# Gathering experts' tokens by an indirect transfer from GpSimd instead of by matmuls with one-hot columns

## The reference

```
scores = softmax(xf @ router_w)                      # 384 tokens, 16 experts
best_group = argmax(sum of the 2 best in each group of 4)
idx = top_k(scores inside the best group, 2)         # two experts per token
gates = scores[idx] / sum(scores[idx])
for each expert e, over the tokens sent to it (x):
    y = (silu(x @ w1[e]) * (x @ w3[e])) @ w2[e]      # three 1024 x 1024 matrices
out[token] += gate * y
```

## Time and profile before

| | |
|---|---|
| median of 3 runs | 1675.11 us |
| the profiled execution, its own time | 1676.27 us |
| its span in the profile | 1674.5 us |
| mean granted TensorE clock | 0.972 |
| busy: PE / DVE / ACT / POOL | 93% / 43% / 20% / 0% |
| DMA | 495.66 MB, mean 296 GB/s |
| chain that ended last | PE 83%, DVE 6%, DMA 5%, ACT 3%, issue 2% |

### The profile page before, as it was taken

The page is one execution under the profiler, slowest core; times in us unless marked ns, Lnnn a source line. Parts: engine busy times, 40 slices in busy tenths (PEclk is TensorE's granted clock), DMA queues, the critical chain, the costliest instruction groups (busy, mean ns, idle before and its releaser), DMA issues.

```text
span 1674.5 us, 21517 instructions
## 1 busy us (share of the span) xinstructions
PE 1555.0 (93%) x7910; PEld 699.9 (42%) x7911; DVE 713.3 (43%) x2050; ACT 331.6 (20%) x539; POOL 0.2 (0%) x4
## 2 busy tenths in 40 slices
PE   6999999978999999999989799896999998999996
PEld 3454555543343333333333355453333333333333
DVE  3325665352424434334343548725334342434343
ACT  4322222030101111010101357413011110111111
POOL 0000000000000000000000000000000000000000
PEclk9999999989999999999999899997999999999998
DMA  9438776830858999999968501424799995999993
GB/s 351 153 106 299 264 262 226 349 153 1 354 249 336 423 422 422 422 422 422 422 267 350 201 0 51 201 101 163 288 413 422 422 422 240 423 422 421 423 423 132
DMA packets 83949, 495.66 MB, mean 296 GB/s; under 512 B 4465, under 2 KB 21121, under 8 KB 28225
## 3 DMA queue, kind: packets, MB, share of 16 engines
q1 hardware_dynamic: 82432, 489.33, 72.3%
q10 hardware_dynamic: 1472, 5.72, 1.0%
HBM read 493.45 MB, written 1.58 MB: 296 GB/s over the span
## 4 chain that ended last, share of the span: by engine, by line
PE 83%; DVE 6%; DMA 5%; ACT 3%; issue 2%; SPq 0%; DVEq 0%; ACTq 0%
PE PS L752 81%; DMA halves<-in_moe_w 4%; PE PS L756 2%; DMA halves<-in_ada_w 1%; DVE misc L1760 1%; ACT hT L543 1%; DVE xc L1702 1%; DVE misc L1522 0%; DVE halves L1522 0%; DVE halves L1513 0%; DVE halves L1515 0%; DVE halves L1514 0%; DVE hT L1750 0%; ACT hT L528 0%; ACT hT L514 0%
## 5 line engine op out<-in xcount | busy, mean ns | idle before, releaser
L752 PE MATMUL PS<-halves,hT 128*64 128x512 f32 x3072 | 677.0, 596 | 22.4 <-ACT hT L543 17.2
L752 PEld LDWEIGHTS PS<-halves,hT 128*64 128x64 f32 x3072 | 225.4, 137 | 442.5 <-issue 432.8
L752 PE MATMUL PS<-hT,halves 128*128 128x384 f32 x640 | 218.7, 497 | 8.4 <-ACT halves L626 6.5
L1702 DVE SCALAR_TENSOR_TENSOR xc<-PS,MOD,xc 128x128 f32<-128x128 f32 x592 | 195.8, 409 | 37.4 <-PE PS L752 37.4
L752 PEld LDWEIGHTS PS<-hT,halves 128*128 128x128 f32 x640 | 121.5, 193 | 106.7 <-issue 23.0
L1750 DVE TENSOR_TENSOR hT<-hT,PS 128x512 f32<-128x512 f32 x32 | 22.0, 688 | 279.3 <-ACT hT L528 279.3
L752 PE MATMUL PS<-halves 128*128 128x384 f32 (+1 forms) x336 | 118.5, 512 | 0.7 <-ACT pre L573 0.7
L752 PE MATMUL PS<-h,hT 128*64 128x512 f32 x408 | 108.8, 667 | 7.4 <-issue 3.9
L1760 DVE COPY misc<-PS 128x512 f32<-128x512 f32 x32 | 22.1, 692 | 216.6 <-PE PS L752 216.6
L528 ACT ACTIVATE hT<-PS 128x512 f32<-128x512 f32 x32 | 19.1, 597 | 449.6 <-PE PS L752 449.6
L752 PE MATMUL PS<-hT,misc 64*128 64x384 f32 x512 | 91.2, 495 | 3.6
(11 more groups left out here) (232 smaller groups left out, 1107.5 us busy)
## 6 DMA issues: line engine op xcount, KB each, us to landing
halves<-in_moe_w SPq DMA_DIRECT2D x192, 2048.0 KB, 16.4
halves<-in_ada_w SPq DMA_DIRECT2D x48, 1024.0 KB, 6.9
halves<-in_hy_w_in SPq DMA_DIRECT2D x12, 1024.0 KB, 5.2
halves<-in_rg_w_in SPq DMA_DIRECT2D x4, 2048.0 KB, 15.5
halves<-in_hy_w_out SPq DMA_DIRECT2D x4, 1024.0 KB, 8.2
halves<-in_rg_w_out SPq DMA_DIRECT2D x2, 2048.0 KB, 9.7
halves<-in_rg_wa SPq DMA_DIRECT2D x1, 2048.0 KB, 11.4
halves<-in_rg_wx SPq DMA_DIRECT2D x1, 2048.0 KB, 15.2
```

The source lines that it names most:

```text
L752: return nc.tensor.matmul(out, lhsT, rhs, start=start, stop=stop)
L1702: ins = v.scalar_tensor_tensor(xc[:, k, cs], PS[:, bank, cs], MOD[:, l, 8 * G2 + k, s:s + 1], xc[:, k, cs], ALU.mult, ALU.add)
```

## The change

Four things are changed, all in the mixture of experts.

**The gather.** At the start of each layer GpSimd stores `h` in a tensor in HBM, `tokens`, in rows of 512 values (2 KB), two rows per token. For experts 1 to 16 of a layer the six gather matmuls are gone. In their place TensorE does three matmuls of `pick`, now 128 wide (the 64 slots twice), with a constant column that holds twice each token's number; VectorE adds 1 on the upper 64 partitions and converts to integers (two instructions of one column); and GpSimd starts an indirect transfer that reads the 128 named rows into `xg`. TensorE's `xg` transposes wait for that transfer (`xg_in`) instead of for VectorE's copy. For each layer's expert 0 the matmul gather stays.

**First and third matrices in fours.** The loads of w1 and w3 take four matrix rows for each partition, contiguous in HBM (16 KB), where they took two blocks of two rows (8 KB). The channels of a token are stored in `tokens` in the order that this needs: ScalarE's `token_tile` writes them permuted. The bytes are the same, and w2 is loaded as before.

**Further passes' outputs in eight banks.** The eight combine matmuls of a further pass go to eight different banks and wait for no addition in between (they wait for `hid`, which frees banks 2 and 3). After them TensorE waits for the fourth addition or a later one (`8 * n + 5`), where it waited for the second or a later one; and the wait for all eight additions stands before the base pass's combine matmuls, no longer before the `hid` transposes.

**`w13_last`** is now counted up by the first of the three small matmuls.

```diff
-        pick = cut(hT, 0, NT * BASE).rearrange("p (t r) -> p t r", t=NT)
+        pick = stack[:, 0, :].rearrange("p (t r) -> p t r", t=NT)
+        rows_f = stack[:, 1, 0:1]
+        rows_i = stack[:, 1, 1:2].bitcast(mybir.dt.uint32)
+        tokens = [nc.dram_tensor(f"tokens{l}", (2 * N, HALF), F32, kind="Internal").ap() for l in range(LAYERS)]
...
-                w = {m: A[m].rearrange("l e (k p j) n -> p (l e) k (j n)", p=P, j=2) for m in ("moe_w1", "moe_w3", "moe_w2")}
+                w = {m: A[m].rearrange("l e (k p j) n -> p (l e) k (j n)", p=P, j=j)
+                     for m, j in (("moe_w1", 4), ("moe_w3", 4), ("moe_w2", 2))}
...
+                    a.activation(h[:, i // 2, i % 2 * HALF:i % 2 * HALF + HALF].rearrange("p (k c) -> p k c", k=4),
+                                 PS[:, 2 + i, :].rearrange("p (c k) -> p k c", k=4), ACT.Copy).then_inc(S("tok"), 1)
...
+        @block.gpsimd
+        def _(pool_):
+            for l in range(LAYERS):
+                for t in range(NT):
+                    pool_.wait_ge(S("tok"), before("tok", l) + 2 * t + 2)
+                    pool_.dma_start(tokens[l][2 * P * t:2 * P * t + 2 * P, :].rearrange("(p j) c -> p (j c)", j=2),
+                                    h[:, t, :]).then_inc(S("tok_out"), 16)
+                pool_.wait_ge(S("tok_out"), 16 * NT * (l + 1))
+                for e in range(NE):
+                    pool_.wait_ge(S("rows"), before("rows", l) + e + 1)
+                    pool_.wait_ge(S("xT_mm"), before("xT_mm", l) + e + 1)
+                    pool_.indirect_dma_start(xg, None, tokens[l], bass.IndirectOffsetOnAxis(rows_i, 0)) \
+                        .then_inc(S("xg_in"), 16)
...
                     pe.wait_ge(S("x_gpT"), n + 1)
-                    for i, (k, bank) in enumerate(X_COMBINE):
+                    pe.wait_ge(S("hid"), before("hid", l) + e + 1)
+                    for k, bank in X_COMBINE:
                         g, kk = k // 2, k % 2
-                        if i >= 6:
-                            pe.wait_ge(S("x_acc"), 8 * n + i - 2)
                         mm(PS[:, bank, 0:N], Xyo[...], XgpT[...], True, True).then_inc(S("x_c_mm"), 1)
-                    pe.wait_ge(S("x_acc"), 8 * n + 3)
+                    pe.wait_ge(S("x_acc"), 8 * n + 5)
...
-                        gather(l, 0, 2, pick, HALF, S("w13_last")).then_inc(S("G_mm"), 1)
+                        for t in range(NT):
+                            last = mm(PS[:, 0, 0:1], pick[:, t, :], const("token_rows")[:, t:t + 1], t == 0, t == NT - 1)
+                            if t == 0:
+                                last.then_inc(S("w13_last"), 1)
+                        last.then_inc(S("G_mm"), 1)
                         pe.wait_ge(S("hid"), before("hid", l) + e + 1)
-                        pe.wait_ge(S("x_acc"), 8 * (done + extra) + 1)
...
-                        pe.wait_ge(S("xg"), before("xg", l) + e + 2)
+                        pe.wait_ge(S("xg_in"), 16 * NE * l + 16 + e * 16)
...
+                        pe.wait_ge(S("x_acc"), 8 * (done + extra) + 1)
                         for k, bank in COMBINE:
...
-                    one_hot(pick, base_iota, cols[:, 0:3], None, BASE, "pick")
+                    one_hot(pick, base_iota, cols[:, 0:3], None, 2 * BASE, "pick")
...
-                    v.tensor_copy(xg, PS[:, 0, :]).then_inc(S("xg"), 1)
+                    ch.link(v.tensor_scalar(rows_f, PS[:, 0, 0:1], const("upper"), None, ALU.add))
+                    v.tensor_copy(rows_i, rows_f).then_inc(S("rows"), 1)
...
-X_COMBINE = ((0, 4), (2, 0), (4, 5), (6, 7), (1, 6), (3, 1), (5, 5), (7, 7))
+X_COMBINE = ((0, 4), (2, 0), (4, 5), (6, 6), (1, 7), (3, 1), (5, 2), (7, 3))
```

More of the change, by code:

```diff
@@ L126 @@
 PER = dict(sq=8, ss_mm=1, rms=1, rinv=1, rb_mm=1, nrm=8, hT_act=BY_ACT, hT_dve=KD - BY_ACT, ada_mm=12, o_mm=8, x_upd=8,
-           rt_mm=3, rt_ev=1, rt_exp=1, rt_max=1, rt_mask=1, tok_mm=6, tok=6, route=1, pick=17, gpick=17, G_mm=17, xg=17,
+           rt_mm=3, rt_ev=1, rt_exp=1, rt_max=1, rt_mask=1, tok_mm=6, tok=6, route=1, pick=17, gpick=17, G_mm=17, xg=1, rows=16,
            xT_mm=17, xT=17, w13_mm=16, sig=16, hid=16, gpT_mm=16, gpT=16, hidT_mm=16, hidT=16, w2_mm=16, yo=16,
@@ L421, in expert @@
                     name, half = order[c]
-                    return w[name][:, l * NE:(l + 1) * NE][:, bass.ds(e, 1), 2 * half:2 * half + 2, :]
+                    n = w[name].shape[2] // 2
+                    return w[name][:, l * NE:(l + 1) * NE][:, bass.ds(e, 1), n * half:n * half + n, :]
                 def load_expert(c, r, e, *released):
                     slot = moe_slot(r, c)
-                    load(("moe", l, slot), expert(c, e), ring[:, slot, :].rearrange("p (o k n) -> p o k n", o=1, k=2),
+                    load(("moe", l, slot), expert(c, e), ring[:, slot, :].rearrange("p (o k n) -> p o k n", o=1, k=1 if c < 4 else 2),
                          *released)
@@ L1063, in chunk, with gather @@
                 return rows[:, 2 * P * (c // 2):2 * P * (c // 2) + 2 * P].rearrange("p (c j) -> p j c", j=2)[:, c % 2, :]
-            def gather(l, bank, groups, picked, width, begun=None):
+            def gather(l, bank, groups, picked, width):
                 m = P // groups
@@ L1069, in gather @@
                     for g in range(groups):
-                        last = mm(PS[m * g:m * g + m, bank, 0:width], picked[:, t, :],
+                        last = mm(PS[m * g:m * g + m, bank, 0:width], picked[:, t, 0:m],
                                   h[:, t, width * g:width * g + width], t == 0, t == NT - 1)
-                        if begun is not None and t == g == 0:
-                            last.then_inc(begun, 1)
                 return last
@@ L1099, in extra_pass @@
                     for c in range(2):
-                        last = tr(PS[:, 1, P * c:P * c + P], chunk(Xxg, c))
+                        last = tr(PS[:, 1, P * c:P * c + P], Xxg[:, P * c:P * c + P])
                     last.then_inc(S("x_xT_mm"), 1)
@@ L1135, in expert_layer @@
                 for c in range(4):
-                    last = tr(PS[:, 1, P * c:P * c + P], chunk(xg, c))
+                    last = tr(PS[:, 1, P * c:P * c + P], xg[:, P * c:P * c + P])
                 last.then_inc(S("xT_mm"), 1)
```

10 lines of the change are left out of this document (5 added, 5 removed).

## The result

The changed kernel takes 1685.55 us (median of 6 runs, 1684.38 to 1687.64) and the kernel before 1676.51 us (6 runs, 1672.68 to 1679.12) on the same chip: ratio 1.0057, 95% interval 1.0044 to 1.0069. The profiled execution took 1684.38 us, its span is 1682.6 us at a mean granted clock of 0.954 (before: 1674.5 us at 0.972).

The account below looks back on a forecast made before the run. TensorE (28.7 us an expert) and weight loads (29.8) were taken to bound the kernel in turn. Layer 0's -5.7 and layer 1's -1.4 plus 2 for the clock gave 1670 us; own range 1664 to 1676, 8 in 10 1657 to 1712.

Parts of the forecast that it names:

- I add 2: Term for TensorE's new 1.4 us idle before hid in each expert: clock falls add 2 us to the whole time.
- dear loads: Rival in the experts' loads: large rows no faster and a gather costs 1.0 us; 1683 us, chance 0.13.
- late transfer: Rival at the indirect transfer: it takes 10.3 us, making an expert 30.3 us; 1711 us, chance 0.21.
- The gather removed: Step between w13 and the transposes: removing 2.75 us of matmuls saves 0.33 us an expert, the rest becomes waiting.
- The transfer added: Step for xg: transfer takes 8.4 us, on time in plain experts, 3.2 us late behind further passes.
- The loads: Step for expert weights: large rows -0.32 us, gather +0.68, so 30.2 us an expert, and loads lead nearly everywhere.
- Further passes: Step from a pass's additions to w2: w2 starts 4.2 us earlier (5.7 in expert 2), less 3.2 for lateness.
- Clock: Step for TensorE's idle before hid: a fall to 1.2 GHz costs 2.5 us, partly hidden; 2 us added in all.
- rival 4: Rival in the experts: the clock falls in most, 30.9 us each, +45 us, 1714 us; chance 0.06.
- rival 1: The late transfer: 10.3 us, row by row between 16 KB rows, +36 us, 1711 us; chance 0.21.
- the short one: Rival at the indirect transfer: at most 5.2 us, so layer 0's three 3.2 us delays go; 1660 us, chance 0.18.
- Layer 0 and layer 1: Sums over each layer's experts and passes: -5.7 us in layer 0 and -1.4 us in layer 1, together -7.1.

Follow-up runs that it names:

- early_fill: Changed kernel with the small matmuls moved into w13, row numbers made before the sigmoid wait, and a 512-column filler in their old place: 1699.69 us, ratio 1.0139.
- fill_short: Changed kernel with three unused matmuls of 224 moving columns before the wait for hid in experts without a further pass: 1680.96 us, ratio 1.0018.
- fill: Changed kernel with three unused matmuls of 448 moving columns before the wait for hid in experts without a further pass: 1688.55 us, ratio 1.0070.
- narrow: Changed kernel with the matmul gather back but one column per matmul, no indirect transfer or GpSimd work, wrong tokens: 1678.62 us, ratio 1.0012.
- rows_first: Changed kernel with the short filler, and with small matmuls and row numbers ahead of a further pass instead of behind it: 1673.19 us, ratio 0.9975.

## Why the prediction was wrong

The forecast was 1670 us, the result lies on the other side of the kernel before. The step that failed is the clock, the term "I add 2"; the further passes' 4.2 us, which rest on the same clock, failed with it. That 1685.55 lies within the range of 8 in 10 (1657 to 1712) and near the 1683 of *dear loads* is luck: the upper end was set by the late transfer at 10.3 us, and neither that nor dear loads came.

*The gather removed*: right. 0.33 us an expert forecast, 0.28 measured where the clock holds: the transposes start 16.10 us behind w13's start instead of 16.47, and the moved wait of the eight banks, which the sum left out, takes 0.09 back. The rest of its 2.75 us became idle time. (32 gathers are gone, as the 32 transfers show, not 30.)

*The transfer added*: right. 8.4 us were taken, 8.3 is the median. In plain experts it is on time or up to 0.4 us late. Behind the five passes TensorE waits 1.5, 2.3, 2.4, 0.9 and 0.2 us for it where 3.2 were forecast; it is less also because w2 lasts 7.8 to 9.2 us there. The Trainium skill's rule ("DMA: Bandwidth & Descriptors", Queues, rings and completion order), by which the eight rows would pass in one turn, does not show here in the form of a short transfer: it is 3.1 us once no load is in flight, and beside loads it grows with the loads' rows, 6.9 us at 8 KB and 8.3 with four of six loads at 16 KB. That growth alone does not refute the rule, since one whole turn of the loads' queue would grow with its rows too. For the other rule ("SBUF — State Buffer", SBUF: two separate sides) the traces show no sign: GpSimd's instruction lasts 0.95 to 1.01 us in all 32 experts, with `gpick` beside it, and as long in early_fill, where it stands beside w13. Whether `gpick` runs in such a mode no row shows.

*The loads*: right in their rate. 16 KB rows make 29.82 us an expert into 12.58 MB / 426 GB/s = 29.5, the gather's 0.26 MB make that 12.85 / 426 = 30.2, the number forecast. But that they *lead nearly everywhere* needs a TensorE at 28.4, and TensorE was at 29.6 on average (experts 4 to 12 of layer 0). Even in fill_short, with TensorE at 28.45, they lead only in experts 9 to 13 of layer 0 and in three of layer 1.

*Further passes*: the step was too large. From the combine matmuls (848.15) to w2 (854.84) are 6.69 us, 6.3 were forecast. Yet only 1.4 us of the 4.2 arrive at that w2's end. It lasts 7.99 us, partly at the lower clock, where it was 7.09; and within the pass a fall stretches 64 matmuls to 5.39 us, which took 3.71 before. In expert 7 of layer 1 it is the other way round, 3.70 us now and 5.39 before, and 3.0 us arrive. Before (L752) and now (L777):

```profile
841.18 3.71 PE PS L752 x64
...
1399.07 5.39 PE PS L752 x64
```
```profile
842.26 5.39 PE PS L777 x64
...
856.45 8.69 DMA hT<-tokens,stack
...
1404.70 3.70 PE PS L777 x64
```

What the step overlooked stands in its own rows: the gather behind expert 0's pass took 4.33 us, a plain one 2.75. The clock was low there before (granted 0.74 from 419.0 to 425.6 us), and the step counts the slow gather as saved. With the gather gone a fall meets w2 instead, 9.22 us behind expert 0's pass where it was 7.09. In expert 1 of layer 0 it is the same: w2 starts 4.5 us earlier after w13, where 4.3 were forecast, but lasts 8.42 us, and 1.3 us more go to the transfer that is late behind expert 0, so 1.9 us are left at w2's end.

So behind expert 2's pass the loads restarted 3.6 us earlier than before, where 7.5 was forecast.

*Clock*: the step that failed. "I add 2" in all; the falls cost TensorE 14 x 1.69 us in plain experts and part of one more, some 25 us, and with those behind passes and in expert 1s the w13 and w2 take 32.5 us more. The mechanism stood as rival 4 with a chance of 0.06 and a price that was too high: a fall costs 1.7 us, not the 2.5 read off a whole gather in the earlier trace rows, and it hits 14 of 25 experts, each then at 30.1 us, not 30.9. (Its +45 is added to the forecast, while rival 1's +36 is added to the kernel before.) The row was there, one fall after 1.99 us and none after 1.94, in two places; the change made 27 such places, and the sum took them as if nearly none would fall. That the fall follows the emptied place is shown by fill and fill_short (filled, with the transfer: none of 25) and narrow (idle, no transfer: 15). In fill_short TensorE then waits for loads in eight experts, and of the 25 us about 12 come back: 4.6 in the time, and 7.3 by an estimate, which its two longer expert 1s take. Without these it would be at 1673.7; no run shows that.

*Rivals 1 to 3*: the late transfer at 10.3 us did not come, nor did the short one, and the loads were not dear (30.2 us an expert, as forecast).

*Layer 0 and layer 1*: -5.7 and -1.4 forecast, +0.5 and +8.7 measured. Layer 1 has fewer passes to gain in, more falls (8 and a part against 6), and no waits for loads before that could go.

## What to carry to other kernels

Work that TensorE does while it waits for another engine is worth less than its duration, and taking it away can cost more than it gives: here the clock of the matmuls behind the emptied place fell in more than half of the plain experts. Where the clock is already low in the rows of the kernel before, a step that takes those matmuls out must ask which ones the fall will meet then. Before you move work off TensorE, ask at each place whether anything hides there, and move it only where nothing does (here behind the five further passes, not in the 27 plain experts). Two limits that lie 1 to 2 us apart pass the lead to each other, so a kernel that frees one of them must be measured with the other's waits in view.

## What the runs showed of the hardware

- 1.38 us of idle TensorE between one-column matmuls and transposes were followed by a w2 of 8.8 us instead of 7.1 (granted clock 0.79 in a window of 8 us around it) in 14 of 25 plain experts, and 1.85 us of it in 15 of 25 of a kernel without the transfer. With 224-column matmuls in that place, and 0.10 us idle, there was no fall in the 25.
- An indirect transfer of 128 rows of 2 KB takes 3.1 us alone, 6.9 us beside loads with rows of 8 KB and 8.3 us where four of six loads have rows of 16 KB; GpSimd is busy 0.95 us with it. It slows an expert's six loads by 0.7 us (29.5 to 30.2).
- Three fp32 matmuls of 64 weight columns and 448 moving (six records) take 2.47 us; six of 512 (twelve records), in pairs on the two halves of the array, 2.75 us.
- At the first run of new instructions in expert 1 TensorE stood still for 1.7 to 5.6 us, at times in the middle of a group of matmuls, with no wait in the profile: about 2 us in the kernel before and in the changed one, 5.57 us in rows_first. What sets it stays open.
